# Later joins in an attention stage, and GpSimd subtractions in 256-column instructions: a two-block network in float32 precision on one core

## The chip, the cores and the metric

The kernel runs on one core of one Trainium2 chip. The metric is the device time of one execution in microseconds (us); lower is better. For the kernel before there are three runs and one profiled execution. All four have the same program and the same inputs.

## The reference

The program computes, for 256 tokens of width 1024, a first block of two layers (differential attention with a gated feed-forward network, then a short gated convolution with another) and a second block (mLSTM heads and stick-breaking heads side by side, cross attention to 256 memory tokens, and a product-key expert layer). Cut to what matters here:

```python
# differential attention, 8 heads, 128-query blocks
s = einsum('bqhcd,bkhcd->bhcqk', q_blk, k)            # c = 0, 1: two score maps per head
p = softmax(where(mask, s, NEG_INF), axis=-1)
a = p[:, :, 0] - lam * p[:, :, 1]
o = einsum('bhqk,bkhe->bqhe', a, v)
o = rms_norm(o, g_sub) * (1.0 - lam_init)             # per token and head
m = o.reshape(B, S, ATTN_WIDTH) @ w_o
...
# expert layer: 128 picks of 16384 experts per token (8 heads x 16)
act = gelu(einsum('cd,ced->ce', xb, u[eb])) * gb
y = einsum('ce,ced->cd', act, v[eb])
```

Every product is wanted at float32 precision.

## The kernel before, in words

**Engines.** TensorE (PE) multiplies, ScalarE (ACT), VectorE (DVE) and GpSimd (POOL) prepare, SyncE (SP) and POOL start transfers. Each engine has its own list of instructions, and they meet at counting semaphores. The order on each engine is the order in which the Python code issues it; nothing reorders it later.

**Three products for one.** A weight or activation w is used as wH, a copy rounded to the format `fp32r` that PE takes, and wL = raw − wH. A product x·w is made of three matmuls: xH·wH, xL·wH and xH·wL. Weights come as chunks of 128x2048 (`raw`, 3 buffers); ACT makes `wH` (line 1002), and `wL` is made by DVE (line 1535) or by GpSimd (function `split` in the gpsimd part, line 2257; the instruction is at line 2265). The table `POOL_LOW` says whose a chunk is: GpSimd has most of the chunks of the attention stage, the first three chunks of each feed-forward, convolution and peer-query stage, every second one of the mLSTM stage, and those of cross attention; 35 whole ones and 24 halves of 1024 columns (`PARTS` is 2 for some chunks), each with one subtraction and one increment of `s_log`. `wH` and `wL` have 3 buffers each.

**Attention** runs in a loop of 20 steps, written out on PE, ACT and DVE. One unit is a head and a block of 128 queries, 16 units in all. In step u PE turns unit u−2 (`att_turn`, transposes of Am through `transpose`, line 403), makes the scores of unit u (`att_scores`, line 556), perhaps a join, then takes `FEED[u]` pieces of filler work (projections of other heads, of memory keys and values, and the first output projection: lines 414 to 416 and 438), and last multiplies unit u−2 with V (`att_out`, line 580). DVE's part of a unit is mask and maximum (`Sm`, lines 1654 and 1656), two scalings, and Am (line 1668). ACT's part is the exponential (line 1108), the transposed copy (line 1115), and the copy of the output into `Og` (line 1120) with its sum of squares (line 1121, into `junk`).

**Norm and join.** Four units make a group g, with buffer `Og[g % 2]`. `att_norm(g)` on DVE (line 1675) scales the group's four blocks by their root mean square and the gain; `att_join(g)` turns them on PE (four transposes at line 403 into bank 6, after waiting for the norm), ACT takes oH from the bank, and DVE makes oL (line 1680), which frees bank 6 for the next `att_turn`. Norms stand in steps 6, 10, 14, 18 and joins in steps 7, 11, 15, 19.

**The expert layer** goes over 128 experts for "in" and 128 for "out". For expert n, ACT makes uH (128x1024, line 1462) as soon as the buffer is free (3 buffers), and uL = raw − uH is made by GpSimd for the even ones of the first 128 (`usplit`, line 2299, 64 in all) and by DVE for all others (line 2058). PE takes 24 matmuls for an expert (lines 942 to 944). In between, DVE finds the top 16 of each half (`route`: lines 2069 to 2154, among them the `eq` steps of 128x2048 at lines 2142 and 2149) and makes the one-hot tables (`hots`: oE, oB and three oA, lines 2202 to 2207). In the "out" half GpSimd makes `ga` in instructions of 256 columns (line 2307).

Of the kernel before, what the change touches and what calls it, by code (L numbers as in the profile page):

```python
# [8 lines left out]
F32 = mybir.dt.float32  # L9
# [12 lines left out]
NR = 3  # L22
NS = 3
NG = 3
UW = 1024
UR = 4
US = 3
# [4 lines left out]
LAM0 = 0.2  # L32
NEG = -3.0e38
PAUSE = 2
BASE = 16512

GAINS = ["mem", "ln1g0", "ln1b0", "ln2g0", "ln2b0", "ln1g1", "ln1b1", "ln2g1", "ln2b1",
# [1 line left out]


FEED = (2, 2, 2, 2, 2, 2, 1, 1, 1, 1, 1, 1, 1, 1, 1, 1, 1, 1, 1, 1)
MFEED = (1, 1, 0, 1, 0, 1, 1, 1, 0, 1, 0, 1)

MEMORY = [("xk", i) for i in range(4)] + [("xv", i) for i in range(4)]
# [108 lines left out]
def build(nc, a, out, ctx):  # L153
# [22 lines left out]
    raw = [sb(f"raw{i}", [P, CW]) for i in range(2)]  # L176
# [215 lines left out]
    def tensor(e):  # L392
# [166 lines left out]
        def att_turn(u):  # L559
            hd, j = UNITS[u]  # L560
            b, i = 6 + u % 2, u % 2
            e.wait_ge(s_Am, u + 1)
            if u < 2:
                e.wait_ge(s_qkT, 2 * TURNED[1, 0] + u + 1)
            elif u >= 6 and u % 4 == 2:
                e.wait_ge(s_oL, u // 4)
            else:
                e.wait_ge(s_Os, u - 1)
            for k in range(j + 1):
                r = transpose(ps[b][:, k * P:k * P + P], Am[i][:, k * P:k * P + P])  # L570
            r.then_inc(s_apt, 1)
# [11 lines left out]
        def att_join(g):  # L583
            b = 6
            e.wait_ge(s_on, g + 1)
            e.wait_ge(s_Os, 4 * g + 5 if g < 3 else 15)
            for n in range(4):
                r = transpose(ps[b][:, n * P:n * P + P], Og[g % 2][:, n, :])
            r.then_inc(s_ojn, 1)
# [29 lines left out]
        for u in range(20):  # L619
            if 2 <= u < 18:  # L620
                att_turn(u - 2)
            if u < 16:
                att_scores(u)
            if u >= 7 and u % 4 == 3:
                att_join(u // 4 - 1)
            for _ in range(FEED[u]):
                next(fill)
            if 2 <= u < 18:
                att_out(u - 2)
# [358 lines left out]
    def scalar(e):  # L988
# [134 lines left out]
        def att_norm(g):  # L1123
            e.wait_ge(s_Os, 4 * g + 4)
            root(ss[g % 2][:, 1, :], ss[g % 2][:, 0, :], 1.0 / P, 0, s_atr)

        def att_join(g):
            e.wait_ge(s_ojn, g + 1)
            e.activation(oH[:, 2 * g:2 * g + 2, :], halves(ps[6]), ACT.Copy).then_inc(s_oH, 1)
# [30 lines left out]
        for u in range(20):  # L1160
            if 2 <= u < 18:
                att_turn(u - 2)
            if u < 16:
                att_scores(u)
            if u >= 6 and u % 4 == 2:
                att_norm(u // 4 - 1)
            if u >= 7 and u % 4 == 3:
                att_join(u // 4 - 1)
            for _ in range(FEED[u]):
                next(fill)  # L1170
            if 2 <= u < 18:
                att_out(u - 2)
# [348 lines left out]
    def vector(e):  # L1521
# [148 lines left out]
        def att_norm(g):  # L1670
            s = ss[g % 2]
            e.wait_ge(s_atr, g + 1)
            e.wait_ge(s_dv, lam_sub)
            for n in range(4):
                r = e.scalar_tensor_tensor(Og[g % 2][:, n, :], Og[g % 2][:, n, :], s[:, 1, n:n + 1], sub[:, :], ALU.mult, ALU.mult)
            r.then_inc(s_on, 1)

        def att_join(g):
            e.wait_ge(s_oH, g + 1)
            e.tensor_tensor(oL[:, 2 * g:2 * g + 2, :], halves(ps[6]), oH[:, 2 * g:2 * g + 2, :].bitcast(F32), ALU.subtract).then_inc(s_oL, 1)  # L1680
# [25 lines left out]
        for u in range(20):  # L1706
            if u < 16:
                att_scores(u)
            if u >= 6 and u % 4 == 2:
                att_norm(u // 4 - 1)  # L1710
            if u >= 7 and u % 4 == 3:
                att_join(u // 4 - 1)
            for _ in range(FEED[u]):
                next(fill)
        whole(fill)
# [533 lines left out]
    def gpsimd(e):  # L2249
        def gain(n, after=None):  # L2250
            if n >= len(GAINS):
                return
            if after is not None:
                e.wait_ge(after[0], after[1])
            e.dma_start(gn[n % NG][:, :], a["gains"][n:n + 1, :].broadcast_to([P, D])).then_inc(s_gn[n % NG], 16)

        def split(lo, hi):

            for n in range(lo, hi):
                if not POOL_LOW[n]:  # L2260
                    continue
                for p in range(PARTS[n]):
                    c = part_cols(n, p)
                    e.wait_ge(s_hi, HI[n] + p + 1)
                    e.tensor_tensor(wL[n % NS][:, c], raw[n % NR][:, c], wH[n % NS][:, c].bitcast(F32), ALU.subtract).then_inc(s_log, 1)  # L2265

        e.wait_ge(s_raw[2], 16)
        for n in range(NG):
            gain(n)
        gain(3, (s_nrm, 4 * RM_MEM + 4))  # L2270
        cut = [0, first("gu0") + 1, first("cin") + 1, first("gu1") + 1, first("win") - 1, first("win"), NCH]
        split(cut[0], cut[1])
        gain(4, (s_ln, 4 * LN_A0 + 4))
        gain(5)
        split(cut[1], cut[2])
        gain(6, (s_ln, 4 * LN_F0 + 4))
        gain(7)
        e.dma_start(cw[:, :, :], a["convw"]).then_inc(s_cw, 16)
        split(cut[2], cut[3])
        gain(8, (s_ln, 4 * LN_A1 + 4))  # L2280
        gain(9)
        split(cut[3], cut[4])
        sig, v = row_done(R_DN1, "dn1", 3)
        e.wait_ge(sig, v)
        e.dma_start(ct[:, :, :], a["conv4"]).then_inc(s_c4, 16)
        e.dma_start(gwt[:, :, :], a["gatew"]).then_inc(s_gw, 16)
        e.dma_start(gbt[:, :], a["gateb"]).then_inc(s_gw, 16)
        e.dma_start(selt[:, :, :], a["sel"]).then_inc(s_gw, 16)
        split(cut[4], cut[5])
        gain(12, (s_nrm, 4 * RM_MIX + 4))  # L2290
        gain(10)
        gain(11)
        split(cut[5], cut[6])


        def usplit(n):
            k = n % UR
            e.wait_ge(s_uh, n + 1)
            e.tensor_tensor(uL[n % US][:, :], raw[k // 2][:, (k % 2) * UW:(k % 2) * UW + UW], uH[n % US][:, :].bitcast(F32), ALU.subtract).then_inc(s_ulg, 1)  # L2299

        def expert_gate(i):
            e.wait_ge(s_rb[i % 4], 16 * (i // 4 + 1))
            if i == 0:
                e.wait_ge(s_G, NB)
            if i >= NA:
                e.wait_ge(s_gL, i - NA + 1)
            e.tensor_tensor(halves(ga[i % NA][:, :]), halves(st[i % 4][:, :]), G[:, :, i, :], ALU.mult).then_inc(s_ga, 1)  # L2307

        usplit(0)
        e.wait_ge(s_used, NCH - 1)  # L2310
        e.iota(iob[:, :], [[1, P]], base=0, channel_multiplier=0, allow_small_or_imprecise_dtypes=True).then_inc(s_iob, 1)
        for n in range(2, P, 2):
            usplit(n)
        for i in range(P):
            expert_gate(i)
# [183 lines left out]
```

## Time and profile before

| | us |
|---|---|
| three runs | 1761.64, 1763.98, 1764.99 |
| their median | 1763.98 |
| profiled execution | 1759.78 |
| its span in the profile | 1757.7 |
| mean granted clock of PE | 0.983 of full speed |

The profiled execution is 4.20 us below the median and its span is 2.1 us shorter than its own time. The profile names an instruction by engine, line, operation and the names of its operands. "Idle before, releaser" is how long the engine stood still just before an instruction and which other instruction's end let it go. A form such as 128x2048 is partitions by elements.

### The profile page before, as it was taken

The numbers are of one execution on the slowest core, as the hardware profiler recorded it, in microseconds if no ns is written. First come the engines' busy times: TensorE is split into PE (matmuls) and PEld (weight loads), VectorE is DVE, ScalarE is ACT, GpSimd is POOL, SyncE is SP. The second block draws the span as 40 slices with busy tenths as digits, with TensorE's granted clock in tenths as the row PEclk, the third lists the DMA queues.
The fourth block names the chain that finished last, engine by engine and source line by source line (L and its number), as shares of the span: only waits on it lengthen the run. The fifth ranks groups of instructions, "written<-read, shape, count | busy, mean of one in ns | idle before, by whom it ended". The sixth has DMA issues, their size and how long they took to land.

```text
span 1757.7 us, 29006 instructions
## 1 busy us (share of the span) xinstructions
PE 1675.6 (95%) x11486; PEld 1528.5 (87%) x11486; DVE 1094.3 (62%) x1769; ACT 851.7 (48%) x1254; POOL 507.9 (29%) x274
## 2 busy tenths in 40 slices
PE   7979999999999998987999999998999999999997
PEld 5767999899899988865889999998999888888886
DVE  5665455466555546673234588998999565555555
ACT  5555444343544444653444454453455455445553
POOL 0645100040400024222441344435433332222221
PEclk9999999999999999988999999999999999999999
DMA  8333655554555545332334576665656677777774
GB/s 326 139 120 125 210 178 183 200 204 171 204 182 190 192 169 183 141 120 72 120 124 155 192 223 214 194 208 169 191 181 184 202 253 242 243 242 242 239 242 174
DMA packets 98069, 331.66 MB, mean 189 GB/s; under 512 B 10972, under 2 KB 44284, under 8 KB 79376
## 3 DMA queue, kind: packets, MB, share of 16 engines
q1 hardware_dynamic: 95904, 322.94, 54.6%
q0 software_dynamic: 2032, 6.89, 1.1%
q8 instruction: 91, 1.49, 0.3%
q14 instruction: 42, 0.34, 0.1%
HBM read 310.91 MB, written 18.87 MB: 188 GB/s over the span
## 4 chain that ended last, share of the span: by engine, by line
PE 83%; DVE 9%; ACT 4%; issue 2%; DMA 2%; POOL 1%; DVEq 0%; SPq 0%; ACTq 0%; POOLq 0%
PE banks L977 19%; PE banks L466 11%; PE banks L414 8%; PE banks L415 8%; PE banks L416 8%; PE banks L942 7%; PE banks L944 6%; PE banks L943 6%; PE banks L438 3%; PE banks L931 2%; ACT wH L1002 1%; DVE wL L1535 1%; DVE qm L1862 1%; PE banks L403 1%; POOL uL L2299 1%
## 5 line engine op out<-in xcount | busy, mean ns | idle before, releaser
L2265 POOL TENSOR_TENSOR wL<-raw,wH 128x2048 fp32r<-128x2048 f32 (+1 forms) x59 | 221.0, 3758 | 627.2 <-ACT wH L1002 627.2
L2058 DVE TENSOR_TENSOR uL<-raw,uH 128x1024 fp32r<-128x1024 f32 x192 | 244.2, 1272 | 201.5 <-ACT uH L1462 201.4
L414 PE MATMUL banks<-xH,wH 128*128 128x256 f32 x1216 | 344.0, 283 | 10.0 <-DVE xL L1562 10.0
L1462 ACT ACTIVATE uH<-raw 128x1024 fp32r<-128x1024 f32 x256 | 270.1, 1056 | 165.1 <-PE banks L977 165.1
L415 PE MATMUL banks<-xL,wH 128*128 128x256 f32 x1216 | 343.0, 282 | 0.0
L416 PE MATMUL banks<-xH,wL 128*128 128x256 f32 x1216 | 342.9, 282 | 0.0
L1535 DVE TENSOR_TENSOR wL<-raw,wH 128x2048 fp32r<-128x2048 f32 (+1 forms) x95 | 217.0, 2286 | 153.1 <-ACT wH L1002 152.9
L1002 ACT ACTIVATE wH<-raw 128x2048 fp32r<-128x2048 f32 (+1 forms) x154 | 269.9, 1762 | 79.4 <-PE banks L466 67.7
L942 PE MATMUL banks<-xH,uH 128*128 128x256 f32 x1024 | 295.9, 289 | 11.0 <-POOL uL L2299 8.9
L943 PE MATMUL banks<-xL,uH 128*128 128x256 f32 x1024 | 289.4, 283 | 0.0
L944 PE MATMUL banks<-xH,uL 128*128 128x256 f32 x1024 | 289.3, 283 | 0.0
L2299 POOL TENSOR_TENSOR uL<-raw,uH 128x1024 fp32r<-128x1024 f32 x64 | 177.5, 2774 | 294.8 <-ACT uH L1462 294.8
L414 PEld LDWEIGHTS banks<-xH,wH 128*128 128x128 f32 x1216 | 229.6, 189 | 11.5 <-issue 11.4
L416 PEld LDWEIGHTS banks<-xH,wL 128*128 128x128 f32 x1216 | 229.7, 189 | 0.0
L415 PEld LDWEIGHTS banks<-xL,wH 128*128 128x128 f32 x1216 | 229.7, 189 | 0.0
L942 PEld LDWEIGHTS banks<-xH,uH 128*128 128x128 f32 x1024 | 194.4, 190 | 11.8 <-POOL uL L2299 9.5
L943 PEld LDWEIGHTS banks<-xL,uH 128*128 128x128 f32 x1024 | 194.5, 190 | 0.0
L944 PEld LDWEIGHTS banks<-xH,uL 128*128 128x128 f32 x1024 | 194.2, 190 | 0.0
L2307 POOL TENSOR_TENSOR ga<-st,G 128x256 f32<-128x256 f32 x128 | 99.1, 775 | 247.1 <-DVE gL L2214 231.2
L977 PE MATMUL banks<-uH,gH 128*128 128x512 f32 x512 | 157.9, 390 | 2.5 <-DVE gL L2214 2.5
L977 PE MATMUL banks<-uL,gH 128*128 128x512 f32 x512 | 157.7, 389 | 0.0
L977 PE MATMUL banks<-uH,gL 128*128 128x512 f32 x512 | 157.6, 389 | 0.0
(318 smaller groups left out, 2610.3 us busy)
## 6 DMA issues: line engine op xcount, KB each, us to landing
raw<-in_eu SPq DMA_DIRECT2D x128, 512.0 KB, 3.8
raw<-in_ev SPq DMA_DIRECT2D x128, 512.0 KB, 3.4
raw<-in_gu SPq DMA_DIRECT2D x44, 1024.0 KB, 4.7
raw<-in_dn SPq DMA_DIRECT2D x22, 1024.0 KB, 4.7
gelu_scratch<-st SPq DMA_DIRECT2D x128, 128.0 KB, 3.6
st<-gelu_scratch SPq DMA_DIRECT2D x128, 128.0 KB, 3.3
raw<-in_win SPq DMA_DIRECT2D x14, 1024.0 KB, 4.9
raw<-in_qkv SPq DMA_DIRECT2D x12, 1024.0 KB, 6.3
```

The lines of the kernel that those rows point to most:

```text
L414: e.matmul(o, wh[:, w0:w0 + P], H[:, k, :], start=k == 0, stop=False)
L415: e.matmul(o, wh[:, w0:w0 + P], L[:, k, :], start=False, stop=False)
L416: t = e.matmul(o, wl[:, w0:w0 + P], H[:, k, :], start=False, stop=k == KT - 1)
L942: e.matmul(ps[b][:, 0:S], wh[:, kc], xH[:, k, :], start=k == 0, stop=False)
L943: e.matmul(ps[b][:, 0:S], wh[:, kc], xL[:, k, :], start=False, stop=False)
L944: r = e.matmul(ps[b][:, 0:S], wl[:, kc], xH[:, k, :], start=False, stop=k == KT - 1)
L977: r = e.matmul(ps[2 * t + q][:, :], l[i % NA][:, ts], w[:, q * 512:q * 512 + 512], start=i == 0 and m == 0, stop=i == P - 1 and m == 2)
L1002: e.activation(wH[n % NS][:, c], raw[n % NR][:, c], ACT.Copy).then_inc(s_hi, 1)
L1462: e.activation(uH[n % US][:, :], raw[k // 2][:, (k % 2) * UW:(k % 2) * UW + UW], ACT.Copy).then_inc(s_uh, 1)
L1535: e.tensor_tensor(wL[n % NS][:, c], raw[n % NR][:, c], wH[n % NS][:, c].bitcast(F32), ALU.subtract).then_inc(s_lov, 1)
L2058: e.tensor_tensor(uL[n % US][:, :], raw[k // 2][:, (k % 2) * UW:(k % 2) * UW + UW], uH[n % US][:, :].bitcast(F32), ALU.subtract).then_inc( ...
L2265: e.tensor_tensor(wL[n % NS][:, c], raw[n % NR][:, c], wH[n % NS][:, c].bitcast(F32), ALU.subtract).then_inc(s_log, 1)
```

## The change

Three things, in one step.

- **Norms.** A table `NORM_AT` sets them in steps 7, 11, 15 and 18: the first three one step later, the last where it was.
- **Joins.** A table `JOIN_AT` sets them in steps 9, 13, 17 and 19: the first three two steps later. `att_turn` waits for oL in steps whose unit is a multiple of 4 from 8 on (units 8 and 12), no longer in units 6, 10 and 14. `att_join` waits for two more of ACT's output copies, and the last one for oL of the join before.
- **GpSimd.** wL and uL are made in instructions of 256 columns (`PW`): a chunk in 8 instead of 1, a half chunk in 4, uL in 4. Only the last increments the semaphore. What is computed is the same.

```diff
+PW = 256
+NORM_AT = {7: 0, 11: 1, 15: 2, 18: 3}
+JOIN_AT = {9: 0, 13: 1, 17: 2, 19: 3}
...
         def att_turn(u):
...
-            elif u >= 6 and u % 4 == 2:
-                e.wait_ge(s_oL, u // 4)
+            elif u >= 8 and u % 4 == 0:
+                e.wait_ge(s_oL, u // 4 - 1)
             else:
                 e.wait_ge(s_Os, u - 1)
...
         def att_join(g):
             b = 6
             e.wait_ge(s_on, g + 1)
-            e.wait_ge(s_Os, 4 * g + 5 if g < 3 else 15)
+            e.wait_ge(s_Os, min(4 * g + 7, 15))
+            if g == 3:
+                e.wait_ge(s_oL, 3)
...
-            if u >= 7 and u % 4 == 3:
-                att_join(u // 4 - 1)
+            if u in JOIN_AT:
+                att_join(JOIN_AT[u])
...
-            if u >= 6 and u % 4 == 2:
-                att_norm(u // 4 - 1)
+            if u in NORM_AT:
+                att_norm(NORM_AT[u])
...
         def split(lo, hi):
...
-                    e.tensor_tensor(wL[n % NS][:, c], raw[n % NR][:, c], wH[n % NS][:, c].bitcast(F32), ALU.subtract).then_inc(s_log, 1)
+                    for c0 in range(c.start, c.stop, PW):
+                        d = slice(c0, c0 + PW)
+                        r = e.tensor_tensor(wL[n % NS][:, d], raw[n % NR][:, d], wH[n % NS][:, d].bitcast(F32), ALU.subtract)
+                    r.then_inc(s_log, 1)
...
         def usplit(n):
             k = n % UR
             e.wait_ge(s_uh, n + 1)
-            e.tensor_tensor(uL[n % US][:, :], raw[k // 2][:, (k % 2) * UW:(k % 2) * UW + UW], uH[n % US][:, :].bitcast(F32), ALU.subtract).then_inc(s_ulg, 1)
+            for c0 in range(0, UW, PW):
+                d = slice(c0, c0 + PW)
+                r = e.tensor_tensor(uL[n % US][:, d], raw[k // 2][:, (k % 2) * UW + c0:(k % 2) * UW + c0 + PW], uH[n % US][:, d].bitcast(F32), ALU.subtract)
+            r.then_inc(s_ulg, 1)
```

PE, first join, before: it stands in step 7, between the scores of unit 7 (QT) and the filler for the heads (Am_94 is unit 5's).

```order
L580 MATMUL banks<-V,AT_87 128x128
L403 MATMUL banks<-ident,Am_94 128x128 x2
L556 MATMUL banks<-KT,QT 128x256 x2
L403 MATMUL banks<-ident,Og_89 128x128 x4
L438 MATMUL banks<-wH_62,xH 128x512
L438 MATMUL banks<-wL_65,xH 128x512
L438 MATMUL banks<-wH_62,xL 128x512
```

PE, first join, now: the same four transposes (line 407 now) stand in step 9, after the turn of unit 7 and the scores of unit 9.

```order
L584 MATMUL banks<-V,AT_87 128x128
L407 MATMUL banks<-ident,Am_94 128x128 x2
L560 MATMUL banks<-KT,QT 128x256 x2
L407 MATMUL banks<-ident,Og_89 128x128 x4
L418 MATMUL banks<-mH,wH_60 128x256
L419 MATMUL banks<-mL,wH_60 128x256
L420 MATMUL banks<-mH,wL_63 128x256
```

Between the two places lie two steps: two more turns, two more pairs of scores, two outputs and the filler of steps 7 and 8.

DVE, first norm, before: it comes right after Am of unit 6, and oL after Am of unit 7.

```order
L1668 SCALAR_TENSOR_TENSOR Am_93<-Sm_85,sm_95 128x128
L1675 SCALAR_TENSOR_TENSOR Og_89<-Og_89,ss_97,sub 128x128 x4
L1654 TENSOR_TENSOR Sm_86<-banks,cst 128x512
L1656 TENSOR_REDUCE sm_96<-Sm_86 128x2
L1658 RECIPROCAL sm_96<-sm_96 128x2
L1661 TENSOR_SCALAR sm_96<-sm_96,lamv 128x1
L1663 TENSOR_SCALAR Sm_86<-Sm_86,sm_96 128x256
L1668 SCALAR_TENSOR_TENSOR Am_94<-Sm_86,sm_96 128x256
L1680 TENSOR_TENSOR oL<-banks,oH 128x512
```

DVE, first norm, now: Am of unit 7 stands ahead of it.

```order
L1674 SCALAR_TENSOR_TENSOR Am_93<-Sm_85,sm_95 128x128
L1660 TENSOR_TENSOR Sm_86<-banks,cst 128x512
L1662 TENSOR_REDUCE sm_96<-Sm_86 128x2
L1664 RECIPROCAL sm_96<-sm_96 128x2
L1667 TENSOR_SCALAR sm_96<-sm_96,lamv 128x1
L1669 TENSOR_SCALAR Sm_86<-Sm_86,sm_96 128x256
L1674 SCALAR_TENSOR_TENSOR Am_94<-Sm_86,sm_96 128x256
L1681 SCALAR_TENSOR_TENSOR Og_89<-Og_89,ss_97,sub 128x128 x4
```

The norm has moved behind one unit's chain, and oL (now line 1686) behind the chains of units 8 and 9.

## Rows read from the trace of the kernel before

**Rows 1.** The page: busy time of each engine, and the chain that ended last.
```profile
PE 1675.6 (95%) x11486; PEld 1528.5 (87%) x11486; DVE 1094.3 (62%) x1769; ACT 851.7 (48%) x1254; POOL 507.9 (29%) x274
...
PE 83%; DVE 9%; ACT 4%; issue 2%; DMA 2%; POOL 1%; DVEq 0%; SPq 0%; ACTq 0%; POOLq 0%
```

**Rows 2.** What PE waited for at 90 to 150 us: total, times, longest.
```profile
PE banks L403 <- DVE Og L1675: 7.1, 1, 7.1
PE banks L403 <- DVE oL L1680: 3.2, 2, 1.7
PE banks L403 <- ACT junk L1121: 1.8, 2, 1.3
```

**Rows 3.** GpSimd's timeline, attention: start, duration, instruction, [idle before].
```profile
78.97 9.18 POOL L2265 TENSOR_TENSOR wL<-raw,wH 128x2048 fp32r<-128x2048 f32 x2 [6.38 <-ACT wH L1002]
93.87 9.43 POOL L2265 TENSOR_TENSOR wL<-raw,wH 128x1024 fp32r<-128x1024 f32 x4 [5.72 <-ACT wH L1002]
```

**Rows 4.** VectorE's timeline of the same time.
```profile
93.21 0.34 DVE L1663 TENSOR_SCALAR Sm<-Sm,sm 128x256 f32<-128x256 f32 x1
...
96.45 2.28 DVE L1663 TENSOR_SCALAR Sm<-Sm,sm 128x128 f32<-128x128 f32 x1
...
101.02 3.21 DVE L1675 SCALAR_TENSOR_TENSOR Og<-Og,ss,sub 128x128 f32<-128x128 f32 x4
```

**Rows 5.** PE's timeline at the first join.
```profile
104.29 1.11 PE L403 MATMUL banks<-ident,Og 128*128 128x128 f32 x4 [7.12 <-DVE Og L1675]
```

**Rows 6.** Windows: length, busy time of PE, PEld, DVE, ACT, POOL; granted clock.
```profile
104.20:107.30 3.10, 3.01 (x10) 2.58 (x11) 1.87 (x6) 1.57 (x5) 0.00 (x0) 0.51 0.90 325
```

**Rows 7.** VectorE and PE in the mLSTM stage.
```profile
810.63 2.74 DVE L1880 SCALAR_TENSOR_TENSOR dn<-dn 128x1 f32<-128x1 f32 x1
...
814.24 0.30 PE L403 MATMUL banks<-ident,Pm 128*128 128x128 f32 x1 [1.94 <-DVE mO L1896]
```

**Rows 8.** GpSimd, VectorE and PE at the start of the first feed-forward stage.
```profile
174.84 9.16 POOL L2265 TENSOR_TENSOR wL<-raw,wH 128x2048 fp32r<-128x2048 f32 x2
...
184.64 2.29 DVE L1535 TENSOR_TENSOR wL<-raw,wH 128x2048 fp32r<-128x2048 f32 x1 [0.35 <-ACT wH L1002]
...
187.01 0.28 PE L414 MATMUL banks<-xH,wH 128*128 128x256 f32 x1
```

**Rows 9.** GpSimd by line: busy, mean ns, idle before.
```profile
L2265 POOL TENSOR_TENSOR wL<-raw,wH 128x2048 fp32r<-128x2048 f32 (+1 forms) x59 | 221.0, 3758 | 627.2 <-ACT wH L1002 627.2
L2299 POOL TENSOR_TENSOR uL<-raw,uH 128x1024 fp32r<-128x1024 f32 x64 | 177.5, 2774 | 294.8 <-ACT uH L1462 294.8
```

**Rows 10.** What PE waited for in the whole span, expert line.
```profile
PE banks L942 <- POOL uL L2299: 8.9, 3, 6.8
```

**Rows 11.** One expert of the steady stretch: GpSimd (and its next), VectorE, ScalarE, PE.
```profile
1129.99 2.38 POOL L2299 TENSOR_TENSOR uL<-raw,uH 128x1024 fp32r<-128x1024 f32 x1 [4.06 <-ACT uH L1462]
1136.43 4.18 POOL L2299 TENSOR_TENSOR uL<-raw,uH 128x1024 fp32r<-128x1024 f32 x1 [4.06 <-ACT uH L1462]
...
1130.44 2.21 DVE L2202 TENSOR_TENSOR oE<-iob,i1T 128x512 bf16<-128x512 bf16 x1
1132.58 0.41 DVE L2204 TENSOR_TENSOR oB<-iob,i2T 128x512 bf16<-128x512 bf16 x1
1132.91 1.08 DVE L2207 TENSOR_TENSOR oA<-oE,gp 128x512 bf16<-128x512 bf16 x3
1133.92 1.21 DVE L2058 TENSOR_TENSOR uL<-raw,uH 128x1024 fp32r<-128x1024 f32 x1
...
1131.71 1.05 ACT L1462 ACTIVATE uH<-raw 128x1024 fp32r<-128x1024 f32 x1
...
1134.82 0.28 PE L942 MATMUL banks<-xH,uH 128*128 128x256 f32 x1
```

**Rows 12.** The eq steps: GpSimd at 1222 us, and a window in which it waited (columns as rows 6).
```profile
1222.14 3.60 POOL L2299 TENSOR_TENSOR uL<-raw,uH 128x1024 fp32r<-128x1024 f32 x1 [3.62 <-ACT uH L1462]
...
1187.92:1197.24 9.32, 4.99 (x48) 4.74 (x47) 9.32 (x14) 3.15 (x5) 9.32 (x1) 0.94 0.33 108
```

More of the change, by code:

```diff
@@ L1164, in scalar @@
                 att_scores(u)
-            if u >= 6 and u % 4 == 2:
-                att_norm(u // 4 - 1)
-            if u >= 7 and u % 4 == 3:
-                att_join(u // 4 - 1)
+            if u in NORM_AT:
+                att_norm(NORM_AT[u])
+            if u in JOIN_AT:
+                att_join(JOIN_AT[u])
             for _ in range(FEED[u]):
@@ L1708, in vector @@
                 att_scores(u)
[L1709 to L1712, printed above, removed]
+            if u in NORM_AT:
+                att_norm(NORM_AT[u])
+            if u in JOIN_AT:
+                att_join(JOIN_AT[u])
             for _ in range(FEED[u]):
```

## The prediction

> **What bounds it now.** The page's first part comes first: PE is busy for 1675.6 of 1757.7 us and holds 83% of the chain that ended last, GpSimd 1% [rows 1]. So time comes only out of the 82 us in which PE stands still, or out of stretches in which it runs at a lower clock. The list of PE's waits, taken for the attention stage, shows what the change aims at: 7.1 us for the norm, 3.2 us for oL in two waits, 1.8 us for ACT in two [rows 2]. The timelines of GpSimd and DVE beside each other tell why the norm is late. GpSimd works from 93.87 to 103.30 on four half chunks of 2.36 us each [rows 3]. DVE's scaling at 96.45 takes 2.28 us where the larger one at 93.21 took 0.34; it ends just behind the end of a half chunk, and the norm at 101.02 ends with the last half chunk [rows 4]. The two engines shut each other out for whole instructions, and DVE gets its turn between two of GpSimd's. PE then waits 7.12 us at the join [rows 5], and for the next 3.10 us its granted clock is 0.51, which is its lower level of 1.2 GHz [rows 6].
>
> **Attention: −11.6.** Removed at most: 7.1 + 3.2 + 1.8 = 12.1 us of waits, and 3.10 × (1 − 0.51) = 1.5 us of slow clock, together 13.6. Two parts of the change cure the long wait, each nearly alone. The pieces: three instructions in a row (scaling, Am, norm) lose about 2 us each to a half chunk, 6 of the 7.1 us. The move: the join comes two steps later, some 12 us (20 steps in 120 us), and the norm only one. So I count the long wait as gone. Of the other 5.0 us I leave 2.0: the distance from a join to the turn that waits for its oL is one step as before, so these waits end only as far as GpSimd caused them. New on PE's path are the join's waits for ACT's copies of units 6, 10 and 14, whose outputs PE made one step before; queued behind the join stand the filler and the output of the step. Bounds: all 5.0 stay (−8.6), or none (−13.6).
>
> **What a piece costs.** One chunk takes 4.59 us (9.16 or 9.18 for two) [rows 3, 8], a uL of half its width 2.38 [rows 11]. The difference is 2.21 us for 1024 columns, hence 0.55 for 256, and 2.38 − 2.21 = 0.17 us is fixed per instruction: 0.72 a piece. A chunk becomes 5.8 us (+1.2), a half chunk or a uL 2.9 (+0.5). Over the 59 subtractions of weights and 64 of experts [rows 9] this is some 90 us more on an engine that is busy for 508 us and idle for the rest; only where PE is near does it count.
>
> **Starts of stages: +2.2.** At the first feed-forward stage GpSimd makes chunks 1 and 2 in 9.16 us from 174.84, to 184.00, and PE needs the second at 187.01, a slack of 3.0 [rows 8]. In pieces it ends at 174.84 + 11.6 = 186.4. DVE's own wL of 2.29 us stands at 184.64 [rows 8]; it now gets in between two pieces, and the end is 188.7, late by 1.7. With three such starts (convolution and second feed-forward besides), of which not all meet a DVE instruction of this size: between 0 and 3 × 2.0 = 6; I take 2.2.
>
> **mLSTM: −1.9.** A one-column instruction of DVE takes 2.74 us at 810.63, and PE waits 1.94 us behind it at 814.24 [rows 7]. It becomes at most a piece, 0.7 us. Bounds −1.9 and 0 (if ACT is late next).
>
> **Experts: +5.4.** PE waits three times for GpSimd's uL, 8.9 us in all, 6.8 the longest [rows 10]. The other two share 2.1 us; one of them, at the start with nothing ahead of it, grows by a uL's 0.5 (taken as 0.4). The steady stretch of 16 pairs (experts 38 to 70) is the large unknown. GpSimd gets uH at 1129.99 and PE wants uL at 1134.82: 4.83 us for 2.38 of work. DVE asks with oE at 1130.44 and is shut out until 1132.4; the next uH, DVE's own, is there at 1131.71 + 1.05 = 1132.76 [rows 11]. In pieces DVE gets in after the first, at 1130.7, and its five instructions take 0.4 + 0.4 + 1.08 = 1.8 us. The neighbour at 1136.43 shows that GpSimd waits through such a run: 4.18 for 2.38 of work [rows 11]. So pieces 2 and 3 end at 1134.0, but DVE's uL (1.2) goes in between at 1133.2, and the last piece ends at 1135.8, late by 0.9. Sixteen times that is 14, the upper bound; the lower is 0, since DVE, no longer held up, comes earlier in the next pairs, before GpSimd has started. I take 3, near the lower end, because an earlier DVE stands idle at its own wait for uH and leaves GpSimd alone. The steps with eq come twice. In the first, +2 (0 to +4, one more instruction of DVE inside two of GpSimd's). In the second stands the long wait: GpSimd is held for 9.32 us while DVE runs 14 instructions without a gap, yet at 1222.14 it waited only 3.60 − 2.38 = 1.2 us and got in [rows 12]. Where a run begins is chance, so the wait may vanish (−6.8) or come again with another piece (+10); I take 0. 0.4 + 3 + 2 + 0 = 5.4.
>
> The Trainium skill, "SBUF — State Buffer", section "SBUF: two separate sides", says that of the pair of ports that DVE and GpSimd share, whoever starts first has it for the whole instruction and the other fully blocks. DVE's rows agree (2.28 instead of 0.34); GpSimd's 9.32 us through 14 instructions is more than the page tells. By its rule alone a waiting piece would wait for one instruction; that is the third rival.
>
> **Sum.** −11.6 + 2.2 − 1.9 + 5.4 = −5.9 against the profiled 1759.78, hence 1753.9. The median of the runs lies 4.2 above that execution, so 1758.1. A measurement of this kernel can tell some 0.2% (3.5 us) from no change.
>
> **Rivals.**
> - *Given back.* The waits are removed, but small ones form in their place: attention at −8.6, starts of stages at +5, experts at +5.4, mLSTM −1.9. That is −0.1: 1763.9. For it: each of these stages has a slack of only some 2 to 3 us. Against it: the 7.12 is far longer than any of them.
> - *GpSimd starves in the expert layer, and it is slower.* A uL now asks four times where it asked once, and each request can meet a run of DVE's instructions. Place: experts 38 to 70; price 0.9 us a pair, 14 instead of 3, which gives −5.9 + 11 = +5.1: 1769.1. It decides from 0.6 us a pair upwards. For it the 4.18 and the 9.32 us; against it the 3.60 and the idle time of an unblocked DVE.
> - *Each piece waits for one instruction at most.* The 9.32 us then becomes 2 or 3, the 6.8 at PE goes, and the steady stretch costs nothing: −5.9 − 6.8 − 3 = −15.7, 1748.3. Against it the same 9.32.
> - *The moves do nothing of their own.* The pieces alone would leave three waits of up to 0.7 us each of the long one, against which the moves are then worth some 2 us; the sum doesn't change by it.
>
> **How the numbers follow.** Forecast 0.47 (its own range −11 to −1, 1753 to 1763): 0.37 faster by over 0.2%, 0.08 within, 0.02 slower. Given back 0.12, all within. Starvation 0.19: 0.17 slower, 0.02 within. Third rival 0.22, all faster. Faster 0.37 + 0.22 = 0.59; within 0.08 + 0.12 + 0.02 = 0.22; slower 0.02 + 0.17 = 0.19. The range goes from the third rival, with 3 us for its own bounds, 1745, to the starvation with a little of the eq steps, 1772.
>
> **What would show it.** Right: no wait for Og over 1 us at 90 to 150 us, no granted clock near 0.5 there, DVE's instructions there under 1.1 us; mean of a wL's pieces 0.7 to 0.8 us; PE at the third chunk of the first feed-forward stage late by 1 to 2 us; the pairs of the steady stretch 6.44 to 6.7 us apart. Wrong: GpSimd's uL waits above 14 us in PE's list (starvation), or under 3 (third rival), or a wait for oL or ACT of over 3 us in all in attention (given back).

## The result, and the profile after

The changed kernel takes 1753.15 us, the median of 4 runs (1752.72 to 1757.28); the kernel before, 1764.49 beside it. The ratio is 0.9943 with a 95% interval from 0.9924 to 0.9963: faster by 0.6%. Measured a second time among the experiments it was 0.9949 (0.9935 to 0.9963). The profiled executions are 1752.72 against 1759.78 us, 7.1 us apart, and it is these 7.1 us that the traces can account for; the medians are further apart (11.3), since before's profiled execution was one of its faster ones.

The page of the changed kernel, first its busy times and the chain:

```profile
PE 1678.9 (96%) x11486; PEld 1531.2 (87%) x11486; DVE 1051.8 (60%) x1769; ACT 851.5 (49%) x1254; POOL 625.6 (36%) x783
...
PE 84%; DVE 5%; ACT 4%; POOL 3%; issue 2%; DMA 1%; SPq 0%; DVEq 0%; ACTq 0%; POOLq 0%
```

DVE's share of the chain has fallen from 9% to 5%, GpSimd's has risen from 1% to 3% [rows 1]. DVE is busy for 42.5 us less, with the same instructions: this was time in which it stood blocked. GpSimd is busy, working or blocked, for 118 us more and gives the same result. By line, with instructions counted and mean ns:

```profile
L2273 POOL TENSOR_TENSOR wL<-raw,wH 128x256 fp32r<-128x256 f32 x376 | 281.3, 785 | 575.3 <-ACT wH L1008 575.1
L2310 POOL TENSOR_TENSOR uL<-raw,uH 128x256 fp32r<-128x256 f32 x256 | 235.2, 949 | 237.1 <-ACT uH L1468 237.1
```

Four pieces of a uL take 3.8 us on average where the whole took 2.77 [rows 9]; 0.7 a piece is work (11.14 us for 16 pieces in a row, shown below), the rest is waiting for DVE.

Both programs have the same 11486 matmuls, so the k-th of one can be set beside the k-th of the other (in attention the change moves some of them, but at the end of the stage the counts are equal again). The table gives how much later (+) or earlier (−) each stretch ended than before, per stretch, in us (first line: where the stretch ends in before):

| kernel | attention | feed-forwards, conv | mLSTM, start | mLSTM, rest, and stick-breaking | cross attention, queries | uL, first | eq, first time | steady pairs | wait at 72 | wait at 78 | rest | all |
|---|---|---|---|---|---|---|---|---|---|---|---|---|
| before, ends at | 172 | 643 | 679 | 830 | 955 | 983 | 1057 | 1189 | 1218 | 1260 | 1746 | |
| changed | −2.7 | −0.4 | −1.4 | −2.9 | +0.5 | +2.5 | +2.7 | +1.5 | −7.1 | +0.9 | −0.7 | −7.1 |

(72 and 78 are numbers of experts, in the second eq steps.) So the forecast was right as a whole, and its largest terms were not. The attention stage, with 13.6 us of waits and slow clock to win back, gave 2.7. Its waits are now these, in the window of rows 2:

```profile
PE banks L407 <- ACT junk L1127: 5.5, 3, 3.0
PE banks L560 <- DVE Sm L1660: 1.7, 1, 1.7
```

The 7.12 us for the norm [rows 5] is gone, and the joins now wait for ACT's copies. Here is the first of them, in the timelines of GpSimd, DVE, ACT and PE:

```profile
97.86 8.80 POOL L2273 TENSOR_TENSOR wL<-raw,wH 128x256 fp32r<-128x256 f32 x12
...
103.77 3.03 DVE L1681 SCALAR_TENSOR_TENSOR Og<-Og,ss,sub 128x128 f32<-128x128 f32 x4
106.73 0.41 DVE L1660 TENSOR_TENSOR Sm<-banks,cst 128x256 f32<-128x256 f32 x1
107.29 0.70 PE L560 MATMUL banks<-KT,QT 64*128 64x256 f32 x4 [1.68 <-DVE Sm L1660]
107.63 0.40 ACT L1114 ACTIVATE Sm<-Sm,sm 128x128 f32<-128x128 f32 x1 [3.87 <-DVE sm L1662]
...
108.41 1.99 ACT L1008 ACTIVATE wH<-raw 128x1024 fp32r<-128x1024 f32 x2
110.31 0.25 ACT L1126 ACTIVATE Og<-banks 128x128 f32<-128x128 f32 x1
...
110.96 1.09 PE L407 MATMUL banks<-ident,Og 128*128 128x128 f32 x4 [2.97 <-ACT junk L1127]
```

Read it from the bottom. The join (PE, line 407) waits 2.97 us for ACT's copy of unit 6, which ACT takes at 110.31, behind 1.99 us of wH, behind an exponential that waited 3.87 us for DVE; and DVE was busy for 3.03 us with the norm, now ahead of the mask. (Which of these sets the wait is tested below.) The norm is four instructions: with GpSimd idle, at the last group of the changed kernel, they take 0.35 us each; here they take 0.80 to 0.83 each, since with GpSimd in pieces each of the four waited for one. In the 3.2 us behind this wait the granted clock is again near its lower level, 0.53, and in the 3.3 us behind the second join, which waits 2.06 us at 131.13, it is at that level, 0.50. In before there is one such stretch at 90 to 150 us [rows 6], here there are two (columns as in rows 6):

```profile
110.90:114.10 3.20, 3.14 (x16) 3.17 (x17) 1.93 (x5) 1.76 (x6) 3.20 (x6) 0.53 0.03 8
131.13:134.40 3.27, 3.27 (x16) 3.27 (x17) 2.05 (x5) 1.72 (x6) 3.27 (x6) 0.50 0.02 5
```

### The profile page after: what moved, and what is told of

The parts are those of the page before. It is cut to its first block, busy times and chain, and to the rows that moved or that the text cites. A ratio compares the mean times of both kernels' runs of the same rounds, so it can differ in the third digit from the quotient of the medians.

```text
span 1750.5 us, 29515 instructions
## 1 busy us (share of the span) xinstructions
PE 1678.9 (96%) x11486; PEld 1531.2 (87%) x11486; DVE 1051.8 (60%) x1769; ACT 851.5 (49%) x1254; POOL 625.6 (36%) x783
## 4 chain that ended last, share of the span: by engine, by line
PE 84%; DVE 5%; ACT 4%; POOL 3%; issue 2%; DMA 1%; SPq 0%; DVEq 0%; ACTq 0%; POOLq 0%
PE banks L983 20%; PE banks L470 12%; PE banks L418 8%; PE banks L420 8%; PE banks L419 8%; PE banks L948 6%; PE banks L950 6%; PE banks L949 6%; PE banks L442 3%; POOL uL L2310 3%; PE banks L937 2%; ACT wH L1008 1%; PE banks L407 1%; DVE wL L1541 1%; DMA raw<-in_qkv 1%
## 5 line engine op out<-in xcount | busy, mean ns | idle before, releaser
L2273 POOL TENSOR_TENSOR wL<-raw,wH 128x256 fp32r<-128x256 f32 x376 | 281.3, 785 | 575.3 <-ACT wH L1008 575.1
L2064 DVE TENSOR_TENSOR uL<-raw,uH 128x1024 fp32r<-128x1024 f32 x192 | 241.9, 1260 | 224.9 <-ACT uH L1468 224.8
L2310 POOL TENSOR_TENSOR uL<-raw,uH 128x256 fp32r<-128x256 f32 x256 | 235.2, 949 | 237.1 <-ACT uH L1468 237.1
L948 PEld LDWEIGHTS banks<-xH,uH 128*128 128x128 f32 x1024 | 194.8, 190 | 11.4 <-POOL uL L2310 11.3
L1486 ACT ACTIVATE st<-banks 128x256 f32<-128x256 f32 x128 | 49.1, 383 | 224.2 <-PE banks L950 224.1
```

Of the source, the lines that this page charges most:

```text
L948: e.matmul(ps[b][:, 0:S], wh[:, kc], xH[:, k, :], start=k == 0, stop=False)
L2273: r = e.tensor_tensor(wL[n % NS][:, d], raw[n % NR][:, d], wH[n % NS][:, d].bitcast(F32), ALU.subtract)
L2310: r = e.tensor_tensor(uL[n % US][:, d], raw[k // 2][:, (k % 2) * UW + c0:(k % 2) * UW + c0 + PW], uH[n % US][:, d].bitcast(F32), ALU.subtract)
```

## The experiments

Every kernel in this section computes the whole reference. The stretches of the table, for all of them (the columns for the mLSTM stage in one, likewise those from 955 to 1189; all against before's trace, the last column the median, with the ratio to before measured beside it and its interval):

| kernel | attention | FF, conv | mLSTM | cross att. | experts to 1189 | 72 | 78 | rest | all | median, ratio |
|---|---|---|---|---|---|---|---|---|---|---|
| changed, again | −2.6 | −0.4 | −4.3 | +1.7 | +6.4 | −7.0 | +0.9 | +0.9 | −4.4 | 1753.4, 0.9949 (0.9935 to 0.9963) |
| moves only | −2.9 | 0 | +1.3 | +1.5 | +0.2 | +1.2 | −0.7 | +0.9 | +1.6 | 1760.6, 0.9988 (0.9976 to 1.0000) |
| pieces only | −4.9 | +1.5 | −2.8 | +0.5 | +6.9 | −7.1 | +7.6 | +1.0 | +2.7 | 1758.5, 0.9979 (0.9966 to 0.9992) |
| wL pieces | −4.9 | +1.5 | −6.0 | +0.5 | +2.2 | +0.4 | 0 | −0.4 | −6.7 | 1753.4, 0.9952 (0.9937 to 0.9967) |
| uL pieces | +2.4 | 0 | +0.8 | −0.1 | +7.0 | −7.1 | +7.5 | +1.8 | +12.4 | 1770.7, 1.0039 (1.0024 to 1.0054) |
| moves, wL pieces | −2.6 | −0.4 | −4.3 | +0.5 | 0 | +0.1 | +1.7 | +1.3 | −3.8 | 1755.5, 0.9965 (0.9952 to 0.9978) |
| joins, wL pieces | −5.4 | +1.5 | −5.9 | +0.5 | +2.3 | +0.4 | 0 | −0.4 | −7.0 | 1752.0, 0.9942 (0.9925 to 0.9958) |
| as moves, wL; ACT's order | −2.9 | −0.4 | −4.2 | +1.7 | −0.1 | +1.3 | 0 | +1.0 | −3.6 | 1755.5, 0.9961 (0.9948 to 0.9973) |
| wL pieces, 72 on DVE | −4.8 | −0.4 | −4.4 | +0.5 | +0.1 | −4.1 | 0 | −0.5 | −13.7 | 1745.8, 0.9923 (0.9903 to 0.9944) |
| all pieces, 72 on DVE | −3.6 | −0.4 | −6.3 | +0.2 | +6.5 | −3.7 | −0.4 | −0.1 | −7.6 | 1753.3, 0.9950 (0.9936 to 0.9963) |
| wL in 512, 72 on DVE | +1.0 | −0.4 | −3.7 | +0.3 | 0 | −4.1 | −0.7 | −0.2 | −7.8 | 1753.1, 0.9951 (0.9937 to 0.9965) |
| joins, wL, 72 and 74 on DVE | −5.3 | −0.4 | −4.4 | +0.5 | 0 | −8.5 | +2.1 | +1.1 | −14.9 | 1744.4, 0.9898 (0.9883 to 0.9913) |

Where nothing of a stretch differs between two kernels it mostly repeats within 0.3 us, but steps of 1 to 3 us come and go (in mLSTM, at the start of cross attention, at the first feed-forward start, and 2 us before 1189 in two kernels). So no single entry below 2 us is built on here unless it repeats. In attention the granted clock makes such steps. With uL's pieces alone, the instructions of this stage are those of before, yet it ends 2.4 us later: its waits are no longer than before's, but PE runs at 0.50 of full speed from 104.41 to 110.30 us, where before does so to 107.2, and the mean granted clock from 95 to 150 us is 0.88 against 0.94. In the same way the stage ends at −3.6 with all pieces and 72 on DVE (0.94) and at −4.8 with wL pieces and 72 on DVE (0.97), with the same waits.

The kernels were measured on three occasions, with before each time (medians 1762.5, 1761.5 and 1762.1 us). So two kernels of different occasions are compared by their ratios and their traces, and not by their medians alone.

### The parts alone

**Moves only.** The tables and waits of the change; both subtractions as before.

> The moves of norms and joins alone; GpSimd's subtractions whole as before. Theory A (either part alone cures the long wait of 7.1 us for the norm, as the prediction said): the wait for Og is gone, new waits of the joins for ACT's copies of 2 to 6 us in all appear, the rest of the program is as before: 3 to 8 us faster than before. Theory B (the pieces do it, the moves only shift waits): the norm and the masks behind it are held by GpSimd's half chunks of 2.4 us, the join waits as long for ACT's copies as before for the norm: within 3 us of before. Expert stage as before in both, with its wait of about 7 us for one uL.

Measured: 1760.6 us, 0.1% faster (0.9988). The wait for Og is gone; in its place stand 5.3 us for ACT in three waits, longest 3.0, and the attention stage gains 2.9. No other stretch gains by more than the scatter. So theory A had the mechanism, but in the medians (1.9 us, with an interval that ends at 1.0000) the moves alone are worth what B gave them.

**Pieces only**, for wL and uL: both loops over 256 columns, with norms and joins in their steps of before.

> 256-column subtractions for wL and uL, norms and joins where they were. Theory A: the long wait for Og falls from 7.1 to 1 to 3 us, oL and ACT waits as before or less: attention 6 to 9 us faster, the other stages as in the changed kernel (together about -4): 9 to 13 us faster than before, so as fast as the changed kernel or up to 2 us faster than it. Theory B': pieces let the norm's four instructions each wait for a piece (as the changed kernel shows, 3.03 us for four), the wait for Og stays at 4 us or more: 5 to 8 us faster.

Measured: 1758.5. In attention the pieces bring 4.9 us, more than the moves (2.9) and more than both together (2.7). But the wait for Og is 3.9 us, not 1 to 3: B', with 4 or more, is nearer. The kernel is 4.0 us faster than before and not 5 to 13; what is missing went at expert 78 (+7.6).

**wL's pieces alone, and uL's pieces alone:**

> 256-column pieces for wL alone, uL whole, norms and joins where they were. If uL's pieces cost (+2.5 at the start of the expert stage, +2.7 in the first eq steps, +1.6 in the steady stretch, as the changed kernel's trace shows against before's, and the long wait of 7 us is chance): this is 3 to 7 us faster than the kernel with both, and the long uL wait of about 7 us in the second eq steps is there or not by chance. If uL's pieces are what removed that wait: this is 0 to 3 us slower than the kernel with both.

> 256-column pieces for uL alone, wL whole, norms and joins where they were. If uL's pieces remove the long wait for good: 0 to 2 us faster than before (-7 against +6.8). If the wait is chance: between 1 faster and 7 us slower than before. Up to the expert stage the trace is before's.

Measured: 1753.4 with wL's pieces, 5.1 us less than with both, and 1770.7 with uL's pieces, slower than before by 0.4%. The first is the first case that was written down, uL's pieces cost; the second, 8.2 us slower, came out worse than any value expected. Of the 12.4 us that its trace shows, 2.4 are the slow clock in attention. For the rest the table says why: they take 7.1 us off the wait at 72, pay 6.9 to 7.0 before it, and in these two kernels make a new wait of the same size at 78:

```profile
1209.76 13.94 POOL L2305 TENSOR_TENSOR uL<-raw,uH 128x256 fp32r<-128x256 f32 x8 [3.09 <-ACT uH L1463]
```

```profile
1221.00 0.58 PE L943 MATMUL banks<-xH,uH 128*128 128x256 f32 x1 [6.25 <-POOL uL L2305]
```

Both are of the kernel with pieces only: GpSimd's timeline (eight pieces, two experts, 13.94 us for some 5.6 of work; one instruction, the first piece, fills the time from 1209.8 to 1218.8) and PE's. Meanwhile DVE runs without a gap; the first and the last of its 14 instructions from the uL at 1208.21 to the third oA:

```profile
1208.21 1.21 DVE L2059 TENSOR_TENSOR uL<-raw,uH 128x1024 fp32r<-128x1024 f32 x1
...
1217.24 1.08 DVE L2208 TENSOR_TENSOR oA<-oE,gp 128x512 bf16<-128x512 bf16 x3
```

### The moves, taken apart

**Moves with wL's pieces**, uL whole:

> The changed kernel with uL whole again (moves and wL's pieces). From the profiles so far: attention as in the changed kernel (-2.7), mLSTM -4 to -5, experts as in before (0), the long uL wait of 6.8 us included: -6.5 to -8 against before's profile. Theory 'moves are harmless': as fast as wL's pieces alone or faster. Theory 'given the pieces, the moves cost some 2 us': 1 to 3 us slower than wL's pieces alone.

**Joins moved, norms not**, with wL's pieces:

```diff
-NORM_AT = {7: 0, 11: 1, 15: 2, 18: 3}
+NORM_AT = {6: 0, 10: 1, 14: 2, 18: 3}
```

> wL's pieces, joins moved as in the change, norms left in steps 6, 10, 14. Theory: the join's new wait for ACT's copy (3.0 us at the first) comes from the norm standing ahead of the mask of the next unit on VectorE, which delays ACT's exponential and the copy behind it. With the norm a step earlier that chain starts earlier: wait 0 to 1 us at the first join, attention -6 to -8, and 2 to 4 us faster than wL's pieces alone. Rival: the wait comes from ACT's wH (2.0 us) that stands ahead of the copy; then it stays at 2 us or more, and the time is that of moves with wL's pieces.

**Moves with wL's pieces, and on ACT the copy ahead of the filler** in the steps before a join:

```diff
+            if u + 1 in JOIN_AT and u < 18:
+                att_out(u - 2)
             for _ in range(FEED[u]):
                 next(fill)
-            if 2 <= u < 18:
+            if 2 <= u < 18 and u + 1 not in JOIN_AT:
                 att_out(u - 2)
```

> Moves and wL's pieces; on ScalarE alone, in the steps before a join (8, 12, 16), the output copy stands ahead of the filler's wH. Rival of the run before (wH ahead of the copy is the cause): the join's wait of 3.0 falls by 2.0 us at the first join and about as much at the second, 3 to 5 us faster than the same kernel without it. If the norm on VectorE is the cause: under 1 us, or slower, since ScalarE now stands idle until PE has made the output and wH comes later.

Measured: 1755.5, 1752.0 and 1755.5 us, beside the 1753.4 of wL's pieces without moves. Given the pieces, the moves as they are cost 2.3 us in attention (−2.6 against −4.9). This repeats: the four traces with wL pieces and both moves end the stage at −2.6 to −2.9, the four with wL pieces and neither at −3.6 to −4.9. The waits at 90 to 150 us differ by 0.6 (7.2 against 6.6); the other part is the clock: with the moves it is at its lower level twice, behind the joins' waits at 110.80 and 131.18, without them once, which is some 1.6 us (estimated from 3.2 us at 0.5). In the medians the cost is 2.2 us too, but there the two intervals overlap. (This trace as a whole is at −3.8 and not at the −6.5 to −8 expected, 1.7 of it at 78 and 1.3 behind it.) With the norms left in place the stage is at −5.4, and PE's wait for the mask falls from 1.7 to 0.4; but the join's wait for ACT stays at 3.0, so the theory that the norm makes it has fallen. The kernel isn't 2 to 4 us faster than wL's pieces alone: it is 0.3 us faster by the traces and 1.3 by the medians, which is within the scatter. With the copy ahead of wH that wait falls, as the rival said. The waits of that kernel in the window of rows 2:

```profile
PE banks L407 <- DVE oL L1688: 3.2, 2, 1.7
PE banks L407 <- ACT junk L1127: 1.8, 3, 1.1
PE banks L560 <- DVE Sm L1662: 1.7, 1, 1.7
```

ACT's three waits fall from 5.5 to 1.8 us, and 3.2 us for oL come back in two waits, as large as in before [rows 2]; the stage ends at −2.9 and nothing is won. The expectation of 3 to 5 us missed. The trace shows why for the first join: PE reaches it 1.9 us earlier (108.91 against 110.80), but on ACT wH and the exponentials still stand ahead of oH, which ends at 112.39 against 112.52; so oL comes as late as before, and PE now waits 1.52 us for it at 114.37. At the end of the attention work, at 149 us, this kernel is 1.6 us ahead of the other, and loses it again before the stage ends; which part of that is owed to the edit isn't shown.

### The long wait, and the size of a piece

**uL of expert 72 by DVE**, with wL's pieces alone. `usplit` and `expert_low` ask a function instead of `n % 2`:

```diff
+UDVE = (72,)
...
+    def on_gp(n):
+        return n < P and n % 2 == 0 and n not in UDVE
```

> wL's pieces alone, and the uL of expert 72, for which PE waited 6.8 us, made by VectorE instead of GpSimd. If the wait is GpSimd held back by a gapless run of VectorE: it goes, VectorE pays 1.2 us in its own order, 5 to 8 us faster than wL's pieces alone. If VectorE's load is the bound there (the steps with eq), the wait comes back under VectorE's name or at the next even expert: within 2 us.

**The same with uL's pieces too:**

> Pieces for wL and uL, norms and joins as before, uL of expert 72 on VectorE. Beside the kernel with wL's pieces alone and the same expert moved (1745.8) it tells the price of uL's pieces without the wait at expert 72. If they cost +2.5 at the start of the stage, +2.7 in the first eq steps and +1.6 in the steady stretch: 7 us slower, 1752 to 1754; if also the wait at expert 78 comes, 1760. If uL's pieces are free apart from chance: 1746.

**wL in pieces of 512**, otherwise as two before:

> wL in pieces of 512 columns instead of 256, the rest as the kernel with wL's pieces alone and uL of expert 72 on VectorE. If what counts is the longest time that GpSimd can hold VectorE (1.2 us instead of 0.7): the norm of four instructions loses at most one piece each, the wait for Og is 4 to 6 us instead of 3.9, mLSTM as before or 1 us worse, the first feed-forward start 1 us better: 0 to 4 us slower than pieces of 256. If the number of instructions counts (each of VectorE's waits for one piece whatever its size, GpSimd's fixed 0.17 us saved): 0 to 2 us faster.

Measured: 1745.8, 1753.3 and 1753.1 us. The first is 7.6 us below the same kernel without the edit in the medians, 5.1 by the ratios, whose intervals overlap, and 7.0 by the traces. Of these 7.0 the edit's own stretch has 4.5 (−4.1 against +0.4): of the 6.8 us PE keeps a wait of 2.62, for the uL of expert 74. Most of the rest is a step of 2.1 us before 1189 that only two kernels have. DVE took on one uL more and PE waited less, so it was GpSimd shut out by DVE, and not DVE's load. Beside it, uL's pieces cost 6.1 us by the traces (6.4 in the stretches up to 1189) and 4.8 by the ratios, whose intervals overlap a little (1752 to 1754 was expected, and the median is there). This is their price when there is no long wait for them to cure. With 512 columns the attention stage ends 5.8 us later than with 256 (+1.0 against −4.8). VectorE's timeline of that kernel has the reason, beside its waits:

```profile
97.12 1.32 DVE L1668 TENSOR_SCALAR Sm<-Sm,sm 128x128 f32<-128x128 f32 x1
98.48 1.26 DVE L1673 SCALAR_TENSOR_TENSOR Am<-Sm,sm 128x128 f32<-128x128 f32 x1
99.67 5.15 DVE L1680 SCALAR_TENSOR_TENSOR Og<-Og,ss,sub 128x128 f32<-128x128 f32 x4
```

```profile
PE banks L408 <- DVE Og L1680: 7.4, 1, 7.4
PE banks L408 <- DVE oL L1685: 3.4, 2, 1.7
```

The norm takes 5.15 us, longer than beside half chunks of 1024 columns (3.21, rows 4), and PE waits for it longer than in before. The expectation had put this wait at 4 to 6 us, with one lost piece at most for each of the norm's instructions, and the kernel at 0 to 4 us slower; the wait is 7.4, and the kernel is slower by 5.9 us in the traces (7.3 in the medians, 4.9 by the ratios). The norm loses a piece of some 1.3 us for each of its four instructions, and the scaling and Am ahead of it lose one each.

### The changed kernel again, and the version that the runs point to

> The changed kernel once more, beside the others. If GpSimd's long waits in the second eq steps depend on the moment at which a piece is asked for, runs of one program may differ: its median lies between 1753 and 1757 (the same program with uL whole has 1755.5), with single runs as much as 8 us apart, since the kernels with uL's pieces and norms and joins as before had a wait of 6.3 us for the uL of expert 78 and this one had none. If the second stall belongs to the order of the program, this one never has it: all runs within 3 us.

Measured: 1753.4, runs from 1751.6 to 1755.7. No run was 8 us away, but they are 4.1 apart and not within 3, so neither case was met as written. The second trace has no wait at 78 either. Of the four traces with uL's pieces and 72 on GpSimd, the two with norms in steps 6, 10 and 14 have that wait, the two of the changed kernel don't. Why moves 1100 us earlier should decide it isn't shown.

**Joins moved, norms not, wL's pieces, uL whole, and 72 and 74 by DVE:**

> The version that the runs point to: wL's pieces, uL whole, joins moved and norms not, uL of experts 72 and 74 on VectorE. From the parts: attention -5.4, mLSTM -4.4, experts -6.8 for 72 and up to -2.6 more for 74 against before's profile: -16 to -19, a median of 1743 to 1746, 0 to 3 us faster than with expert 72 alone. If VectorE becomes the bound at 74 (its eq step and two more uL of 1.2 us): PE waits for VectorE's uL there instead, and it is the 1746 of expert 72 alone.

Measured: 1744.4 us, 0.9898 of before (0.9883 to 0.9913), and 9 us less than the change. PE's waits in the first half of the experts:

```profile
PE banks L952 <- POOL uL L2312: 3.9, 3, 1.8
PE banks L952 <- DVE uL L2068: 2.1, 1, 2.1
```

No wait is longer than 2.1 us there. Of the 8.5 us gained at 72 and 74, 2.1 come back at 78 (1.8 of it a wait for GpSimd). The trace is at −14.9, short of the −16 to −19 expected. Its trace is 1.2 us and its median 1.4 below those of wL pieces with 72 on DVE, which is within the scatter of runs; what moving the joins and expert 74 add isn't shown by that.

## Why the prediction was right, and where it was not

Forecast were 1758.1 us and −5.9; measured are 1753.2, and −7.1 by the two traces. The 4.2 us that the forecast added for the distance from profiled execution to median were 0.4 in the changed kernel. The direction, the range, the price of a piece and the shorter wait in mLSTM held. That the total came out near was luck: attention gave 8.9 us less than forecast, and a wait at expert 72 that had been put at nothing gave 7.1 more.

- **Attention, −11.6: measured −2.7.** This is the step that failed most. "Either part nearly alone cures the long wait" was taken from three instructions each losing 2 us to a half chunk [rows 4]. For single instructions it held: beside pieces no scaling and no Am at the first join takes over 0.9 us. For the norm the row's x4 was read as one instruction; it is four, and each of them now queues for one piece. That makes 3.03 us where the whole half chunks had cost 3.21. Second, the 2.0 us set aside for the waits that stay or are new were 7.2 (5.5 and 1.7). Third, the 1.5 us of slow clock were counted as won, and became some 3.1 (estimated from 3.2 us at 0.53 and 3.27 at 0.50). The text had named the wait for ACT's copy and said only what stands behind it; it should have asked what stands ahead of that copy on ACT, which was 1.99 us of wH and an exponential that waits for DVE.
- **A piece, 0.72 us: measured 0.70.** Two chunks in a row at the first feed-forward start took 11.14 us (forecast 11.6).

```profile
171.62 11.14 POOL L2273 TENSOR_TENSOR wL<-raw,wH 128x256 fp32r<-128x256 f32 x16
```

- **Starts of stages, +2.2: measured −0.4 in the feed-forwards and the convolution.** The step "DVE's wL gets in between two pieces" was wrong. Just before, DVE's fL, 0.43 us when nothing holds it, was held for 3.35 us through GpSimd's last five pieces, and DVE came to wL only when GpSimd was done:

```profile
179.70 3.35 DVE L1762 TENSOR_TENSOR fL<-fv,fH 128x256 fp32r<-128x256 f32 x1 [0.48 <-ACT fH L1205]
182.97 2.28 DVE L1541 TENSOR_TENSOR wL<-raw,wH 128x2048 fp32r<-128x2048 f32 x1
```

- **mLSTM, −1.9: measured −2.9, and −1.4 at its start, which the sum didn't have.** The one-column instruction takes at most 0.28 us now (2.74 in rows 7). At the start it is `xm` for two half rows, 2.38 us instead of 5.70, which shortens the next wait of PE from 3.88 to 1.39:

```profile
654.02 2.38 DVE L1580 SCALAR_TENSOR_TENSOR xm<-h,rs,gn 128x512 f32<-128x512 f32 x2
...
669.56 0.36 PE L418 MATMUL banks<-xH,wH 128*128 128x256 f32 x1 [1.39 <-DVE xL L1568]
```

- **Experts, +5.4: measured about +0.5.** By its parts: the first uL was to cost 0.4 and cost 2.5, since DVE's uL got in between its pieces (four pieces took 3.77 us, and PE waits 2.49). The first eq steps were to cost 2 and cost 2.7. The steady stretch was to cost 3 and cost 1.5, near the lower end for the reason that was given: DVE is done earlier, its uL at 1131.66 stands idle 2.36 us before its uH comes, and a uL of GpSimd's takes 3 to 5.5 us within the 4.83 that it has or little over. The starvation rival, 0.9 us a pair, did not come.

```profile
1128.11 3.86 POOL L2310 TENSOR_TENSOR uL<-raw,uH 128x256 fp32r<-128x256 f32 x4 [1.03 <-ACT uH L1468]
...
1131.66 1.39 DVE L2064 TENSOR_TENSOR uL<-raw,uH 128x1024 fp32r<-128x1024 f32 x1 [2.36 <-ACT uH L1468]
```

- **Second eq steps, 0: measured −7.1 at 72 and +0.9 at 78.** The forecast called it chance, between −6.8 and +10. The pieces shorten the wait at 72 in all four traces that have them for uL with 72 on GpSimd (−7.0 to −7.1), so that end is no chance:

```profile
1187.64 5.70 POOL L2310 TENSOR_TENSOR uL<-raw,uH 128x256 fp32r<-128x256 f32 x4 [1.81 <-ACT uH L1468]
```

  Without this, the change would have been as good as nothing: −7.1 + 7.1. In the changed kernel uL's pieces paid for themselves by it: with uL whole (moves, wL pieces) the trace is at −3.8 against −7.1 and −4.4. At 78 the upper end came true in two kernels (+7.5), and not in the changed one.
- **The third rival** (each piece waits for one instruction at most) named a gain at 72 that came, and there for its reason: the four pieces of the 5.70 us took 1.21, 2.78, 0.92 and 0.90, each behind one DVE instruction. As a rule it failed: with pieces only the first piece of the 13.94 us waits through the run of DVE's instructions, and the steady stretch cost 1.5 and not nothing. By the rule of the Trainium skill, "SBUF — State Buffer", section "SBUF: two separate sides", the one that starts first has the ports for its whole instruction and the other blocks. The traces agree that whole instructions block (0.80 to 0.83 us beside pieces of 0.7, 2.28 beside half chunks); the 9 us of GpSimd's first piece and the 3.35 us of DVE's fL, each through several instructions, are more than it says.
- **Given back, and the signs.** In attention this rival is what happened, and more than it priced (−8.6): its sign, over 3 us of waits for oL or ACT there, came (5.5). Of the forecast's own signs, no wait for Og, pieces of 0.7 to 0.8 us on average (0.785) and pairs some 6.5 us apart in the steady stretch came; no clock near 0.5 and a late third chunk did not, and DVE's instructions stayed under 1.1 us one by one but not as the group of four. The signs of the two other rivals (over 14 us of waits for GpSimd's uL, or under 3) did not come: it is 9.5. For the last rival, that the moves do nothing of their own: alone they gave 1.9 us in the medians, given the pieces they cost 2.3 in attention.

## What to carry to other kernels

Cutting the holder of a shared port into pieces helps a single instruction of the other side by the length of the whole, and a group of n small ones hardly: here each of them paid for one piece, and some single ones for more, so count instructions, not groups, and take n times the length of a piece as the least price. Cut where the other engine is on the critical path (here wL, beside DVE's chains in attention and mLSTM), and leave whole what is itself late (here uL, 5 to 6 us, unless the pieces cure a longer wait). When a wait is moved away from one producer, list what stands ahead of the next one's instruction on its own engine before calling the wait gone.

## What the runs showed of the hardware

DVE, waiting beside back-to-back GpSimd instructions, got in after each one of them at the norm: 3.03 us for four instructions beside pieces of 0.70, 5.15 beside pieces of 512 columns. Elsewhere it didn't: fL, 0.43 us by itself, took 3.35 us through five pieces at 179.70 and 2.23 through three at 473.23, and `yc` of the convolution 2.40 through four at 373.54, and the second trace of the changed kernel has all three again. GpSimd, waiting beside back-to-back DVE instructions, most of them with two inputs, sometimes gets in after one (3.60 us instead of 2.38) and sometimes only when DVE stops: 9.32 us through 14 instructions [rows 12], and 9.14 us for the first of the eight pieces. What decides between the two, for either engine, isn't known from these runs.

The granted clock fell to its lower level, 0.50 to 0.53, behind some of PE's waits (7.12, 2.97 and 2.06 us), and traces with the same instructions differ in how long it stayed there: to 107.2 in before, to 110.3 with uL's pieces.
